# A transformer kernel on one core: 48 of 64 adaLN modulation chunks computed on VectorE in the feed forward loops

## The reference

```python
def adaln(cond, w, b):
    d = w.shape[0]
    m = jax.nn.silu(cond) @ w + b
    return [m[:, None, i * d:(i + 1) * d] for i in range(6)]

def modulate(x, g, shift, scale):
    return rmsnorm(x, g) * (1.0 + scale) + shift

def swiglu(h, wg, wu, wd):
    return (jax.nn.silu(h @ wg) * (h @ wu)) @ wd
...
        sh1, sc1, g1, sh2, sc2, g2 = adaln(c, ada_w, ada_b)
        csh1, csc1, cg1, csh2, csc2, cg2 = adaln(c_ctx[None, :], ada_w, ada_b)
        h = modulate(x, n_mix, sh1, sc1)
        hc = modulate(xc, n_mix, csh1, csc1)
        o, oc = mixer(h, hc, row, col, need_ctx, *mparams)
        x = x + g1 * o
        x = x + g2 * swiglu(modulate(x, n_ffn, sh2, sc2), wg, wu, wd)
        if need_ctx:
            xc = xc + cg1 * oc
            xc = xc + cg2 * swiglu(modulate(xc, n_ffn, csh2, csc2), wg, wu, wd)
```

## Time and profile before

| | |
|---|---|
| time, median of 3 runs | 2675.94 us (2674.3 to 2682.66) |
| span of the profiled execution | 2666.8 us |
| TensorE busy | 2458.1 us, 92% of the span, 23209 matmuls |
| VectorE busy | 1880.0 us, 70% |
| ScalarE busy | 1466.4 us, 55% |
| moved by DMA | 674.38 MB, 253 GB/s over the span |

### The profile page before, as it was taken

How to read it: one execution, slowest core, us unless ns; L and a number is a source line. 1 busy time by engine, 2 the same in 40 slices (tenths; PEclk the granted TensorE clock), 3 DMA queues, 4 the chain that set the end, 5 groups by cost and what they waited for, 6 DMA issues and landing times. The chain is left out here.

```text
span 2666.8 us, 58450 instructions
## 1 busy us (share of the span) xinstructions
PE 2458.1 (92%) x23209; PEld 1851.2 (69%) x23209; DVE 1880.0 (70%) x2489; ACT 1466.4 (55%) x1865; POOL 14.9 (1%) x12
## 2 busy tenths in 40 slices
PE   6988999999898889999899999889999899999997
PEld 4745777677664457768677768667777777777775
DVE  3277555655645566555765555769999999999997
ACT  3146444433421545434454434458888888888885
POOL 0000000000200000000000000000000000000000
PEclk9989999999988999999999999999999999999999
DMA  7340555554456126555375545439999999999995
GB/s 302 116 200 25 223 199 208 214 199 163 150 223 243 75 89 259 207 186 183 140 276 192 210 174 185 163 113 396 411 417 414 417 418 407 419 416 418 418 417 232
DMA packets 121213, 674.38 MB, mean 253 GB/s; under 512 B 13489, under 2 KB 13969, under 8 KB 67089
## 3 DMA queue, kind: packets, MB, share of 16 engines
q1 hardware_dynamic: 120032, 664.47, 64.1%
q10 hardware_dynamic: 1072, 8.42, 0.8%
HBM read 671.79 MB, written 1.05 MB: 252 GB/s over the span
## 5 line engine op out<-in xcount | busy, mean ns | idle before, releaser
L984 PE MATMUL ps<-projected,normed_or_mix 128*128 128x256 bf16 x1504 | 409.9, 273 | 1.5 <-issue 1.5
L985 PE MATMUL ps<-projected,normed_or_mix 128*128 128x256 bf16 x1504 | 409.9, 273 | 0.0
L1383 DVE TENSOR_TENSOR aux<-weights,aux 128x1024 bf16<-128x1024 f32 x223 | 271.2, 1217 | 1.4 <-ACT aux L1329 1.4
L1378 DVE TENSOR_TENSOR turned<-weights,turned 128x2048 bf16<-128x2048 f32 x112 | 256.3, 2288 | 8.9 <-ACT turned L1323 4.2
L1323 ACT ACTIVATE turned<-weights 128x2048 bf16<-128x2048 f32 x112 | 213.6, 1907 | 49.7 <-DMA weights<-moe 47.3
L1329 ACT ACTIVATE aux<-weights 128x1024 bf16<-128x1024 f32 x223 | 232.1, 1041 | 2.1 <-PE ps L1267 1.8
L1254 PE MATMUL ps<-projected,turned 128*128 (+1 forms) x1792 | 232.9, 206 | 0.0
L1253 PE MATMUL ps<-projected,turned 128*128 (+1 forms) x1792 | 232.9, 206 | 0.0
L1255 PE MATMUL ps<-projected,turned 128*128 (+1 forms) x1792 | 232.9, 206 | 0.0
L831 PE MATMUL ps<-weights_halves,normed_or_mix_halves 128*128 128x512 f32 (+4 forms) x576 | 218.6, 380 | 0.0
L1265 PE MATMUL ps<-aux,probs 128*96 128x512 bf16 x448 | 172.6, 385 | 43.4 <-DVE probs L1393 43.4
(11 more groups left out here) (399 smaller groups left out, 6365.8 us busy)
## 6 DMA issues: line engine op xcount, KB each, us to landing
weights<-moe SPq DMA_DIRECT2D x224, 1024.0 KB, 8.5
weights<-moe SPq DMA_DIRECT2D x224, 512.0 KB, 6.6
weights<-l_ffn SPq DMA_DIRECT2D x66, 1024.0 KB, 4.9
weights<-ada SPq DMA_DIRECT2D x64, 1024.0 KB, 5.6
weights<-l_ffn SPq DMA_DIRECT2D x66, 512.0 KB, 5.6
weights<-ada SPq DMA_DIRECT2D x64, 512.0 KB, 6.0
weights<-ffn SPq DMA_DIRECT2D x28, 1024.0 KB, 4.9
weights<-w_in SPq DMA_DIRECT2D x24, 948.0 KB, 4.8
```

The lines of the kernel that those rows point to most:

```text
L984: pe.matmul(o, hi, h_hi(k), start=(k == 0), stop=False)
L985: pe.matmul(o, hi, h_lo(k), start=False, stop=False)
L1378: dve.tensor_tensor(gu4[j % SLOTS][1], RING[:, slot(j), 0:2 * D], gu4[j % SLOTS][0], ALU.subtract).then_inc(front_used.sem, 1)
L1383: dve.tensor_tensor(down4[j % SLOTS][1], RING[:, slot(j), 2 * D:3 * D], down4[j % SLOTS][0], ALU.subtract).then_inc(back_used.sem, 1)
```

## The change

The 48 later chunks leave TensorE, the ring and `plan`. Their weights lie in HBM transposed, as pairs of tiles of 128 output columns by 1024 inputs (`ada_turned`), and the conditions as rows (`conds`). In the dense feed forward loops ScalarE's DMA queue loads such a pair (or half of one) per round into two buffers in turn (`load_side`), and VectorE multiplies it by the silu of the condition, spread over the partitions, and sums along the row in the same instruction, straight into the modulation table (`take_side`). 16 of layer 0's 22 rounds have such work (half a pair with two conditions), 20 of the context's 22, 20 of layer 1's 22, 24 of the first hybrid layer's 28: 80 rounds with two products each. The biases are added behind the last of them (`side_bias`). The row parameters of layer 1 and of the hybrid layers are loaded in the feed forward stage before. For ScalarE and VectorE the dense loops are written out round by round; TensorE keeps its hardware loop. In `modulate`, the transposes use seven PSUM banks where they used five.

```diff
-    planned("ada", 3, 16)
     planned("l0_ffn", F0 // PB)
-    planned("ada", 2, 19)
...
-    def modulate(streams, norm, rows=None, batch=0, gates=(), own=False, begin=(), loads=()):
-
-        bank = lambda k: (k + 2 * len(gates)) % 5
+    def modulate(streams, norm, batch=0, gates=(), begin=(), rows=None, loads=()):
+
+        banks = 5 if begin else 7
+        bank = lambda k: (k + 2 * len(gates)) % banks
...
-                if rows is not None and not begin:
-                    act.dma_start(ROW[:, :], d["rows"][rows].partition_broadcast(PB)).then_inc(rows_in.sem, 16)
...
                 keep_odd(KD)
-                if rows is not None and not begin:
-                    act.wait_ge(rows_in.sem, rows_in.at(16))
...
-            for i in range(ada_n):
-                ada_row(pe, i, ada_at)
-            zero_products(pe, 2 if ada_n else 14, 5)
+            zero_products(pe, 14, 5)
...
             up(0, 0, gates is None)
-            for i in range(ada_n):
-                ada_turn(pe, i)
             with pe.Fori(0, rounds) as g:
...
-            zero_products(pe, max(0, 18 - 8 * behind), 4)
+            zero_products(pe, 18, 4)
...
+        def load_side(act, i):
+            src = side[i][0]
+            act.dma_start(turned_w[i % 2][:, 0:src.shape[1]], src).then_inc(turned_in[i % 2].sem, 16)
...
+                for at, c in silus_of:
+                    act.dma_start(cond_row[at], d["conds"][c].partition_broadcast(PB)).then_inc(cond_in.sem, 16)
+                for i in range(min(2, len(side))):
+                    load_side(act, i)
+                if rows is not None:
+                    act.dma_start(ROW[:, :], d["rows"][rows].partition_broadcast(PB)).then_inc(rows_in.sem, 16)
+                for c in range(n):
+                    silu_of(act, c, c, hid, T)
+                    if c + 2 < n:
+                        cast_hi(act, 0, c + 2, c + 2)
+                    if c + 1 < n:
+                        cast_hi(act, 1, c + 1, c + 1)
+                    for i, (at, _) in enumerate(silus_of) if c == 0 else ():
+                        act.wait_ge(cond_in.sem, cond_in.at(16 * len(silus_of)))
+                        act.activation(cond_row[at], cond_row[at], ACT.Silu).then_inc(cond_made.sem, 1)
+                    if 1 <= c < len(side) - 1:
+                        act.wait_ge(turned_used.sem, turned_used.at(c))
+                        load_side(act, c + 1)
+                if rows is not None:
+                    act.wait_ge(rows_in.sem, rows_in.at(16))
...
+        def take_side(dve, i):
+            src, products = side[i]
+            if i == 0:
+                dve.wait_ge(cond_made.sem, cond_made.at(len(silus_of)))
+            dve.wait_ge(turned_in[i % 2].sem, turned_in[i % 2].at(16 * (i // 2 + 1)))
+            for (at, layer, tile, c, row_), spare_row in zip(products, spare):
+                w = turned_w[i % 2][:, at:at + D]
+                ins = dve.scalar_tensor_tensor(out=spare_row, in0=w, scalar=1.0, in1=cond_row[row_], op0=ALU.mult,
+                                               op1=ALU.mult, accum_out=ADA[:, layer, tile, c:c + 1])
+            ins.then_inc(turned_used.sem, 1)
...
+                for c in range(n):
                     gate_of(dve, c, c, hid, T)
                     if c + 2 < n:
                         make_lo(dve, 0, c + 2, c + 2)
                     if c + 1 < n:
                         make_lo(dve, 1, c + 1, c + 1)
+                    if c < len(side):
+                        take_side(dve, c)
+                    if side and c == len(side):
+                        side_bias(dve)
...
-    ffn(X, F0, 0, behind=3)
+    ffn(X, F0, 0, side=side_work(104, 40, (2,)), silus_of=((0, 2),), rows=2)
...
-        scan_mixer(layer, 6)
+        scan_mixer(layer)
```

More of the change, by code:

```diff
@@ L604, in _ @@
                     sq.then_inc(S.hop_a.sem, 1)
[L605 to L608, removed]
+                    for i in range(early, early + 2):
+                        ada_copies(act, i)
                 act.wait_ge(S.hop_b.sem, S.hop_b.at(1))
@@ L618, in _ @@
                         ada_copies(act, i)
[L619 to L627, removed]
+                for g in range(len(gates)):
+                    keep_gate(act, g, gates)
+                    keep_odd(1)
                 keep_odd(KD)
-                if rows is not None and not begin:
-                    act.wait_ge(rows_in.sem, rows_in.at(16))
             @block.tensor
             def _(pe):
[L634 to L648, removed]
                 def meanwhile():
@@ L1034, in ffn_done, with ffn_parts @@
             s.done(n)
-    def ffn_parts(x, f, o, gates=None, gate=GB, first=0, ada_at=None, ada_n=0, behind=0):
+    def ffn_parts(x, f, o, gates=None, gate=GB, first=0, side=(), silus_of=(), rows=None):
         a, n = place.n, f // PB * (NE if gates is not None else 1)
+        turned_w = [P[:, 4096 + i * 2048:4096 + (i + 1) * 2048] for i in range(2)]
+        spare = [P[:, 2048:3072], P[:, 3072:4096]]
+        squared = P[:, 8192:8704] if gates is None else EX[:, 4096:4608]
+        cond_row = [EX[:, 3072:4096], EX[:, 4096:5120]]
         hid = [PS[:, 4 + p, :] for p in range(2)]
@@ new lines, in side_bias @@
+        def side_bias(dve):
+            dve.wait_ge(turned_used.sem, turned_used.at(len(side)))
+            those = sorted({(layer, c, tile) for _, products in side for _, layer, tile, c, _ in products})
+            runs = []
+            for layer, c, tile in those:
+                if runs and runs[-1][:2] == (layer, c) and runs[-1][3] == tile:
+                    runs[-1] = (layer, c, runs[-1][2], tile + 1)
+                else:
+                    runs.append((layer, c, tile, tile + 1))
+            for layer, c, lo, hi in runs:
+                o = ADA[:, layer, lo:hi, c]
+                dve.tensor_tensor(o, o, col("ada_b", layer * 48 + lo, hi - lo), ALU.add)
@@ L1225, in ffn @@
         S.tail_added.done(4)
+        cond_in.done(16 * len(silus_of))
+        cond_made.done(len(silus_of))
+        for i in range(2):
+            turned_in[i].done(16 * len(side[i::2]))
+        turned_used.done(len(side))
+        if rows is not None:
+            rows_in.done(16)
     def moe_parts(he_hi, he_lo, put_t, fc, turn_put, keep_put):
```

206 lines of the change are left out of this document (63 added, 143 removed).

## The result

| | before | after |
|---|---|---|
| median of the timed runs | 2677.11 us (4 runs, 2674.3 to 2682.66) | 2644.44 us (4 runs, 2636.32 to 2647.95) |
| ratio | | 0.9868, 95% interval 0.9844 to 0.9891 |
| span of the profiled execution | 2666.8 us | 2644.0 us |

The account below looks back on a forecast made before the run. TensorE was taken to bound the dense loops, with the gain at their seams: 34.6 us won less 1 for the clock puts the span at 2633.2, and with 9.1 around it the time at 2642 us, range 2631 to 2666.

Parts of the forecast that it names:

- (1): Layer 1's two head norms, nine chunks each: without the chunks they end 11.09 and 2.88 us earlier, together 13.97.
- (2): Four dense loop prologues: the turns between first and second up product go, 1.26 us each on TensorE, together 5.04.
- (3): Tails of layer 1's and the first hybrid layer's loops: 3.03 us less each before the next stage, together 6.06.
- (4): ScalarE's wait for row parameters closing three modulation stages: loading them a stage earlier saves 2.68, 2.80 and 1.68, together 7.16 us.
- (5): Modulation stages ahead of layer 1's and the first hybrid layer's loops: ScalarE's chunk copies go, 1.17 us each, together 2.34.
- 33.6: The forecast fall of the span in us: 34.6 from the seams less 1 for TensorE's clock.
- (6, 7): Dense rounds: 160 VectorE products and 80 transfers on ScalarE's queue fit the waiting time and cost nothing.
- 3.19 us of room: VectorE's waits in a 7.83 us dense round, 2.60 for ScalarE's silu and 0.59 for its cast, free for the products.
- the lag of 5.7 us a loop: How far VectorE can fall behind in a dense loop before TensorE stops: 5.7 us.
- 9.1 us lie outside the span: Median 2675.94 less the profiled span 2666.8 us was taken as time outside the span and kept unchanged.
- (9): TensorE idling in the head norms may lower its clock behind them: 1 us taken, 8.8 at most.

Follow-up runs that it names:

- before_again: The kernel before, unaltered, run once more for a second trace: 2676.19 us against 2677.76 of the series, ratio 0.9994.
- rows_only: The kernel before with only the row parameter loads of layers 1 to 3 moved to the feed forward stage before: 2676.31 us against 2677.39, ratio 0.9991.
- ffn_only: The kernel before without the 18 chunks of the feed forward stages and the modulation stages ahead of them: 2661.37 us against 2681.23, ratio 0.9931.
- rows_back: The changed kernel with the row parameters of layers 1 to 3 loaded in the modulation stage again: 2649.41 us against 2644.87 unaltered.
- four_products: The changed kernel with four VectorE products instead of two in each of the 80 rounds: 2727.87 us, ratio to before 1.0176.
- again_2: The changed kernel, unaltered, run as the base of a later series: 2644.87 us.
- warm: The changed kernel with zero products on TensorE where the chunks had been in head norms and scans: 2633.27 us, ratio to before 0.9824.
- warm_again: The changed kernel with zero products in head norms and scans, measured a second time: 2632.0 us beside 2644.87 without them, ratio to before 0.983.

## Why the prediction was right, and where it was not

- **The seams** were right. By the rows of after: (1) the head norms, to TensorE's next operation, 10.9 and 2.7, together 13.5 (forecast 13.97); (2) the dense stages shorter by 2.53 (both of layer 0), 1.26 and 1.26, together 5.05 (5.04); (3) 3.02 and 3.01, together 6.03 (6.06); (4) 2.77 + 2.38 + 1.53 = 6.7 (7.16); (5) two modulation stages, from the first scaling of the norm to ScalarE's last copy, from 5.38 to 3.89, 2.98 (2.34). Sum 34.2, where 34.6 was worked out. About 2.5 us more came from seams that were not counted, 0.8 at the context tail and 0.6 in layer 0's modulation stage among them. In (5) the seven banks have a part: ahead of the experts, where no chunk stood, the same stretch went from 4.06 to 3.89; no run here takes the banks alone. And the second head norm was read in a trace in which its chunks cost little: VectorE's wait of 2.64 there is 4.8 in `before_again`, 5.5 in `rows_only` and 5.3 in `ffn_only`. So the seams gave 2 to 5 us more than forecast. The times, 33 to 35 us less in three series, do not show this surplus; something of that size was lost elsewhere (left open below), and that the sum met 33.6 so closely is in part luck.
- **Whose cost it was** was wrong for part of (4): moving the row loads was booked at 7.2 us, but with the chunks gone it is worth 3.2 by the trace of `rows_back` and 4.5, not clear of the scatter, by its times. The sum held, because the chunks' removal brought the remainder.
- **The side work** (6, 7) costs nothing, as forecast: the round is 7.83 us, and leaving the work out changes nothing that can be measured. The 3.19 us of room held to within 0.16 a round; the lag of 5.7 us a loop was too large, by `four_products` it is 2.6, which the two products did not need. The product with its sum takes 1219 + 83 ns, less than the 1283 + 188 that the nearest rows gave. The Trainium skill's rule in "Vector Engine (DVE) Microarchitecture Reference", section "Points that are easy to get wrong", that this operation on two non-bf16 SBUF sources halves throughput, does not show here: 1219 ns stand against 1.22 us of the subtraction of the same size, which has no sum. By that rule the time would have been about that of four products, some 85 us slower.
- **The base** was wrong. "9.1 us lie outside the span" is the step that failed: 1.8 us do, and the profiled execution was some 7 us faster than the median. The span after was forecast at 2633.2 and came at 2644.0, 2642.3 and 2641.1, and around it there are 1.8 us and not 9.1. The forecast time did not suffer, since 2642 is the median less 33.6 wherever the 9.1 lie. A typical span of before, 2675 or so, less 33.6 is 2641 to 2642, so the difference was met and its base wrong. It is also in part why the two first traces differ by 22.8 us only, and `before_again` and `again_2` by 35.8.
- **The clock** (9) was priced at 1, with 8.8 as the bound. Turn and linear behind the first head norm took 31.5 us before and 30.7 after, so nothing was lost there. On the clock of the scans the forecast said nothing. In the seven traces with the change and without zero products the first scan takes 57 us and the second 60 each time; in the five of the kernel before and of it with parts left out or moved, 5 of 10 scans are the longer ones. So the change made long scans no more frequent here; why it is always the second is not shown.
- **Left open**: what moving the rows is worth by the times, and whether the 90 to 96 us of layer 0's attention in the changed kernel, against 89 to 94 before it, are more than chance. `warm` and `warm_again`, with the same code up to there, have about 90, and `rows_only`, without the change, has 94; no run here settles it.

## What to carry to other kernels

Where one engine bounds a loop and another waits a fixed time in every round, work from the seams between the loops can go there at no cost, up to that wait; test it with one piece more and one more again, and the step in the time shows the room. Read a seam in more than one trace before it is priced. Compare medians with medians: one profiled execution may stand at the edge of the scatter, so check its span against the spans of the timed runs before anything is placed outside it. When work is taken off TensorE, look at the granted clock in the stages that it leaves idle.

## What the runs showed of the hardware

- The accumulating product on VectorE is two entries in the trace, 1219 ns and a reading of 83 ns that overlaps the next instruction; two in a row cost 2.28 us.
- The granted clock follows what TensorE does even where TensorE seems to have time: with zero products in its idle stretches the mean clock of the run went from 0.957 to 0.983 and the time down by 9 to 13 us. The Trainium skill ("TensorE: Matmul & The Clock Gate", section "Part 1: The HAM clock gate (the "warmup" mystery)") says that the throttled state is the default and activity releases it; the scans at 0.97 with the zero products and 0.77 to 0.84 without agree with that.
- A scan of the same program takes 56.7 us where the granted clock of its middle 20 us is 1.00 and 60.7 where it is 0.82. The two scans alone move the kernel before by 8 us from one execution to another.
